# A ring of five weight units, stage boundaries that split units ahead of the norm, another opening, and an attention stage with its rotary key on GpSimd

## The reference, cut to what matters

```python
for i in range(DEPTH):
    f = swiglu(rmsnorm(h, ffn1_pre_g[i]), ffn1_w_in[i], ffn1_w_down[i])     # 1024 -> 2 x 2816 -> 1024
    h = h + 0.5 * rmsnorm(f, ffn1_post_g[i])
    hn = rmsnorm(h, mix_pre_g[i])
    if i % 2 == 0:   # gated MLP over chunks beside a state space scan, one output projection
        mixed = jnp.concatenate([ya, yb], axis=-1) @ hyb_w_out[j]
    else:            # latent attention: 16 heads, a rotary key shared by all of them
        mixed = mla_attention(hn, ..., cos, sin)
    h = h + rmsnorm(mixed, mix_post_g[i])
    f = swiglu(rmsnorm(h, ffn2_pre_g[i]), ffn2_w_in[i], ffn2_w_down[i])
    h = h + 0.5 * rmsnorm(f, ffn2_post_g[i])
    gate = jax.nn.sigmoid(rmsnorm(h, ple_pre_g[i]) @ ple_w_gate[i])
    h = h + rmsnorm(gate * (p[i] @ ple_w_proj[i]), ple_post_g[i])
```

## Time and profile before

| | |
|---|---|
| three runs | 1171.07, 1170.84, 1170.70 us (median 1170.84) |
| the profiled execution | 1170.79 us, span 1169.0 |
| granted clock of TensorE, mean over the span | 0.995 of full speed |
| TensorE busy | 1123.9 us, 5780 matmuls |
| VectorE, ScalarE, GpSimd busy | 819.4, 566.4, 114.3 us |
| read from HBM | 204.29 MB, 176 GB/s |

### The profile page before, as it was taken

The page is one execution under the profiler, slowest core; times in us unless marked ns, Lnnn a source line. Parts: engine busy times, 40 slices in busy tenths (PEclk is TensorE's granted clock), DMA queues, the critical chain, the costliest instruction groups (busy, mean ns, idle before and its releaser), DMA issues.

```text
span 1169.0 us, 15408 instructions
## 1 busy us (share of the span) xinstructions
PE 1123.9 (96%) x5780; PEld 945.5 (81%) x5780; DVE 819.4 (70%) x1027; ACT 566.4 (48%) x671; POOL 114.3 (10%) x139
## 2 busy tenths in 40 slices
PE   7999999999899999999998999999989999999997
PEld 4888887788787788888777888887878878888875
DVE  5767777677786677677765777768865576776775
ACT  5444445567433644444555444445554554444453
POOL 4000000201600300000123000003100030000012
PEclk9999999999999999999999999999999999999999
DMA  7654554744342564645455655553622356555441
GB/s 269 239 216 173 186 183 146 283 163 158 112 163 108 186 219 180 213 172 190 154 195 197 216 176 183 184 212 108 216 108 73 109 188 216 178 182 205 166 169 54
DMA packets 30546, 206.05 MB, mean 176 GB/s; under 512 B 3504, under 2 KB 3536, under 8 KB 7072
## 3 DMA queue, kind: packets, MB, share of 16 engines
q1 hardware_dynamic: 27216, 194.00, 46.3%
q0 software_dynamic: 3280, 11.35, 3.0%
HBM read 204.29 MB, written 1.05 MB: 176 GB/s over the span
## 4 chain that ended last, share of the span: by engine, by line
PE 83%; DVE 9%; POOL 2%; ACT 2%; issue 1%; DMA 1%; DVEq 0%; POOLq 0%; ACTq 0%
PE PS L505 23%; PE PS L202 15%; PE PS L203 14%; PE PS L204 14%; PE PS L508 12%; DVE WL L178 4%; DVE hn L341 1%; DVE h L317 1%; DVE X L381 1%; DMA QG<-pre_g 1%; PE PS L354 1%; PE PS L1606 1%; PE PS L1607 1%; ACT junk L271 1%; ACT WH L172 0%
## 5 line engine op out<-in xcount | busy, mean ns | idle before, releaser
L178 DVE TENSOR_TENSOR WL<-raw,WH 128x2048 fp32r<-128x2048 f32 x182 | 418.1, 2299 | 147.2 <-ACT WH L172 147.1
L172 ACT ACTIVATE WH<-raw 128x2048 fp32r<-128x2048 f32 x183 | 349.0, 1908 | 133.5 <-PE PS L204 127.6
L505 PE MATMUL PS<-X,WH 128*128 128x512 f32 x1152 | 288.4, 392 | 0.0
L505 PEld LDWEIGHTS PS<-X,WH 128*128 128x128 f32 x1152 | 209.1, 189 | 39.0 <-DVE actb L619 0.2
L508 PEld LDWEIGHTS PS<-X,WL 128*128 128x128 f32 x1152 | 157.2, 190 | 11.2
L508 PE MATMUL PS<-X,WL 128*128 128x256 f32 x1152 | 160.6, 282 | 0.0
L202 PE MATMUL PS<-WH,X 128*128 128x512 f32 (+1 forms) x352 | 140.6, 400 | 9.1 <-DVE X L381 6.6
L204 PE MATMUL PS<-WL,X 128*128 128x512 f32 (+1 forms) x352 | 137.2, 390 | 0.0
L203 PE MATMUL PS<-WH,X 128*128 128x512 f32 (+1 forms) x352 | 137.1, 389 | 0.0
L202 PE MATMUL PS<-WH,BH 128*128 128x512 f32 x288 | 113.4, 394 | 0.0
L203 PE MATMUL PS<-WH,BL 128*128 128x512 f32 x288 | 112.5, 391 | 0.0
(11 more groups left out here) (265 smaller groups left out, 1365.8 us busy)
## 6 DMA issues: line engine op xcount, KB each, us to landing
raw<-stream SPq DMA_DIRECT2D x183, 1024.0 KB, 4.8
QG<-pre_g POOLq DMA_DIRECT2D x8, 512.0 KB, 8.0
PG<-post_g POOLq DMA_DIRECT2D x8, 512.0 KB, 6.8
h<-x SPq DMA_DIRECT2D x2, 512.0 KB, 7.6
out<-h SPq DMA_DIRECT2D x4, 256.0 KB, 2.0
wsT<-gm_w POOLq DMA_DIRECT2D x1, 512.0 KB, 10.5
gm_g<-gm_g POOLq DMA_DIRECT2D x1, 512.0 KB, 11.0
gm_b<-gm_b POOLq DMA_DIRECT2D x1, 512.0 KB, 13.9
```

Of the source, the lines that this page charges most:

```text
L172: act.activation(WH[:, n % RING, :], raw[:, n % RING, :], ACT.Copy).then_inc(sem("w_hi"), 1)
L178: dve.tensor_tensor(WL[:, n % RING, :], raw[:, n % RING, :], WH[:, n % RING, :], ALU.subtract).then_inc(sem("w_lo"), 1)
L505: pe.matmul(PS[:, bank, :], wh[:, kt, cols], X[:, kt, :, :].rearrange("p a n -> p (a n)"), start=kt == 0, stop=False)
```

## The change

It touches five things.

*The ring.* It has five slots in place of three, and `WL` is placed over the same bytes as `raw`, so the low part is written over the raw data. A load waits until unit n-5 has been used (`w_used`); ACT's split waits for the load alone. The loops of the feed-forward stages are written out; splits come one or two units earlier.

*Boundaries.* On DVE one split goes ahead of `behind` and one between x's low part and the second `behind`; on ACT one more unit is split ahead of x's high part. The sum of the squares' halves (`post_mean`) moves from GpSimd to DVE. After a ple stage the gains no longer wait for the squares. `lagged` takes a lead of 2: second tokens stand two units behind, and their transposes at the third unit (in hybrid by `first_gemms`, the first two projections in one such order). The transposes of the next stage's first tokens come in two halves between the last products. In a ple stage a gate block stands between the two projections; ACT splits up to first+6 before it loads the sigmoid's table, up from first+4.

*The opening.* x is transposed as it is, and the gains are applied by ACT as a scale (`qg_cols`, one column for each 128 of width) when it makes the high part; units 0 and 1 are loaded and split by halves. ACT's first table load stands behind the wait for the transposes and for `qg_cols` in the new order; before it stood ahead of every wait. The idle products start on a `zeros` tile of their own wait, 7 and 8 in place of 16 and 4.

*Attention.* The rotary key is copied by ACT (`krs`) and rotated for both token blocks at once on GpSimd; its transposes come as a piece of their own behind the queries. The half split on GpSimd is gone. The order of pieces is queries, then keys; K2 stands behind the first scores, K3, R1, Q2, Q3 in the first two steps of the head loop. `out_unit(5, 1)` and `out_unit(6, 0)` move to the last steps.

```diff
-RING = 3
+RING = 5
...
+        WL = place("WL", [P, RING, UNIT], f32r, offset=base)
         WH = place("WH", [P, RING, UNIT], f32r)
-        WL = place("WL", [P, RING, UNIT], f32r)
...
-        def load_unit(sp, n, k=None, step=0):
+        def load_unit(sp, n):
             if n >= RING:
-                sp.wait_ge(sem("w_hi"), unit_at(n - RING + 1, k, step))
-                sp.wait_ge(sem("w_lo"), unit_at(n - RING + 1, k, step))
...
-            sp.dma_start(raw[:, n % RING, :], src).then_inc(sem(f"raw{n % RING}"), 16)
...
+                sp.wait_ge(sem("w_used"), n - RING + 1)
+            sp.dma_start(raw[:, n % RING, :], a["stream"][n, :, :]).then_inc(sem(f"raw{n % RING}"), 16)
...
-            if n >= RING:
-                act.wait_ge(sem("w_used"), unit_at(n - RING + 1, k, step))
+            act.wait_ge(sem(f"raw{n % RING}"), 16 * (n // RING + (1 if n % RING > 1 else 0)))
             act.activation(WH[:, n % RING, :], raw[:, n % RING, :], ACT.Copy).then_inc(sem("w_hi"), 1)
...
+        def lagged(units, lead=1):
...
+            order = []
+            for j in range(len(units) + lead):
+                if j < len(units):
+                    order.append((units[j], 0))
+                if j >= lead:
+                    order.append((units[j - lead], 1))
...
+            if stages[s][0] != "ple":
+                dve.wait_ge(sem("post_sq"), 4 * s + 2 * t + b + 1)
...
+        def post_mean(dve, s, t):
+            dve.wait_ge(sem("post_sq"), 4 * s + 2 * t + 2)
+            if stages[s][0] == "ffn":
+                dve.wait_ge(sem("pre_rs"), 2 * s + t + 1)
+            dve.tensor_scalar(col(s, t, POST_RS), col(s, t, POST_SQ), col(s, t, POST_SQ + 1),
+                              col(s, t, POST_EPS) if stages[s][0] == "ffn" else EPS, ALU.add, ALU.add)\
+               .then_inc(sem("post_ms"), 1)
...
+        def first_x_high(act, t, a_):
+            if (t, a_) == (0, 0):
+                act.wait_ge(sem("qg_cols"), 16)
+            act.wait_ge(sem("x_tr"), 2 * t + a_ + 1)
+            for q in range(4):
+                kt = 4 * a_ + q
+                ins = act.activation(XH[:, kt, tok(t)], PS[:, x_bank(0, t, a_), q * P:(q + 1) * P], ACT.Copy,
+                                     scale=qg_cols[:, kt:kt + 1])
+            ins.then_inc(sem("x_hi"), 1)
...
+            split_to(m + 2)
             x_high(act, s, 0)
-            split_to(m + 1)
-            if s:
-                post_square(act, s - 1, 1)
+            post_square(act, s - 1, 1)
             pre_square(act, s, 0)
-            split_to(m + 3 if stages[s][0] == "ple" else m + 2)
+            split_to(m + 3)
...
+        def opening_act(act, done):
+            act.wait_ge(sem("consts"), 1)
+            first_x_high(act, 0, 0)
+            first_part_hi(act, 0, 0)
+            first_x_high(act, 0, 1)
+            first_part_hi(act, 0, 1)
+            pre_square(act, 0, 0)
+            first_part_hi(act, 1, 0)
+            first_x_high(act, 1, 0)
...
+            load_table(act, ACT.Silu)
...
+            split_to(m + 1)
             behind(dve, s - 1, 0)
...
-            split_to(m)
             x_low(dve, s, 0)
-            split_to(m + 1)
+            if stages[s][0] != "mla":
+                split_to(m + 2)
             behind(dve, s - 1, 1)
             x_low(dve, s, 1)
             if stages[s][0] != "mla":
-                split_to(m + 2)
+                split_to(m + 3)
...
+            order = lagged(range(4), 2) if s else [(j, t) for j in range(4) for t in range(2)]
...
+                    if s and (j, t) == (2, 0) and q % 2 == 0:
+                        transpose_x(pe, s, 1, (q // 2,))
...
+            def projected(t, middle=None):
...
-                wide(pe, u, t, 4 + 2 * t, p_hi, p_lo, 0, True, True)
-            for j, t in [(0, 0), (0, 1), (1, 0), (2, 0), (3, 0), (1, 1), (2, 1), (3, 1)]:
+                wide(pe, u, t, 4 + 2 * t, p_hi, p_lo, 0, True, True, middle=middle)
+            def gate(j, t):
                 if j == 0:
                     x_there(pe, s, t, 1)
-                wide(pe, u + 1 + j, t, 2 * t, XH, XL, 2 * j, j == 0, j == 3, "ple_gate" if j == 3 else None,
-                     middle=(lambda: transpose_x(pe, s, 1)) if (j, t) == (0, 0) else None)
+                wide(pe, u + 1 + j, t, 2 * t, XH, XL, 2 * j, j == 0, j == 3, "ple_gate" if j == 3 else None)
+            pe.wait_ge(sem("p_lo"), i + 1)
+            projected(0)
+            gate(0, 0)
+            projected(1, lambda half: transpose_x(pe, s, 1, (half,)))
+            for t in range(2):
+                for j in range(1 - t, 4):
+                    gate(j, t)
...
-            split_to(first[s] + 4)
+            split_to(first[s] + 6)
             load_table(act, ACT.Sigmoid)
         def ple_dve(dve, s, done, split_to):
-            split_to(first[s] + 4)
+            split_to(first[s] + 5)
...
+        ROPE0, V00, V01, ROPE1, V10, V11, Q0, Q1, R0, K0, K1, K2, K3, Q2, R1, Q3 = range(16)
         PIECES = [(PA, "turn", None), (PB, "act", None), (PC, "act", None), (PD, "turn", 2), (PB, "act", None),
-                  (PC, "act", 3), (PA, "act", None), (PB, "dve", None), (PC, "act", None), (PD, "dve", 4),
-                  (PA, "act", None), (PB, "dve", 5), (PC, "act", None), (PD, "dve", None), (PA, "act", None),
-                  (PB, "dve", 6)]
+                  (PC, "act", 3), (PA, "act", None), (PB, "dve", 4), (PA, "act", None), (PC, "act", None),
+                  (PB, "dve", None), (PA, "act", None), (PB, "dve", 5), (PA, "act", None), (PB, "dve", None),
+                  (PB, "act", 6)]
...
+            wait_emptied(K0)
+            pe.wait_ge(sem("ml_krT"), 1)
             scores(0)
             scores(1)
-            turned(Q3, u + 6, 2, 4, 0)
-            wait_emptied(R1)
+            keys(2)
             for j in range(8):
                 if j == 1:
+                    wait_emptied(Q2)
+                if j == 2:
                     wait_emptied(Q3)
                 transpose_probabilities(2 * j)
                 if j < 7:
                     scores(2 * j + 2)
-                if j:
+                if j == 0:
+                    keys(3)
+                if j == 1:
+                    transpose_ropes(1)
+                if 0 < j < 7:
                     out_unit(j - 1, 0)
+                if j == 7:
+                    out_unit(5, 1)
                 transpose_probabilities(2 * j + 1)
                 if j < 7:
                     scores(2 * j + 3)
                 weighted_values(2 * j)
-                if j == 7:
...
-                if j > 1:
+                if j == 0:
+                    queries(2)
+                if j == 1:
+                    queries(3)
+                if 1 < j < 7:
                     out_unit(j - 2, 1)
...
+                weighted_values(2 * j + 1)
+            out_unit(6, 0)
...
             take(V11)
+            take(Q0)
+            split_to(u + 7)
+            rotary_key()
+            take(R0)
             take(K0)
-            split_to(u + 6)
-            take(K2)
-            split_to(u + 7)
-            take(Q0)
-            take(R0)
-            take(Q2)
             load_table(act, ACT.Exp)
...
+            split_to(u + 2)
+            latent_means(0)
             dve.wait_ge(sem("ml_cg"), 32)
             latents(0)
-            dve.wait_ge(sem("ml_half"), 1)
-            split_lo_half(dve, u + 2, 1).then_inc(sem("w_lo"), 1)
-            done[0] = u + 3
             latents_low(0)
             split_to(u + 3)
+            latent_means(1)
             latents(1)
-            split_to(u + 4)
             latents_low(1)
             turn(0)
+            split_to(u + 4)
             turn(1)
             split_to(u + 5)
+            take(Q1)
+            split_to(u + 6)
             take(K1)
-            take(K3)
-            split_to(u + 6)
-            take(Q1)
             split_to(u + 7)
-            take(R1)
+            dve.wait_ge(sem("ml_cm"), 1)
...
+                if j < 2:
+                    take((K3, R1)[j])
+                split_to(u + 7 + j)
...
+            pool.wait_ge(sem("ml_kr"), 2)
+            pool.wait_ge(sem("ml_cn"), 2)
+            x0, x1 = krs[:, :, 0:HALF], krs[:, :, HALF:ROPE]
+            pool.tensor_tensor(kw[:, 0, :, :], x0, cosT[:, :, :], ALU.mult)
+            pool.tensor_tensor(kw[:, 1, :, :], x1, sinT[:, :, :], ALU.mult)
+            pool.tensor_tensor(kw[:, 2, :, :], x1, cosT[:, :, :], ALU.mult)
+            link(pool, "pool_chain", pool.tensor_tensor(kw[:, 3, :, :], x0, sinT[:, :, :], ALU.mult))
+            for twice in range(2):
+                lo = 384 + ROPE * twice
+                pool.tensor_tensor(cn[:, :, lo:lo + HALF], kw[:, 0, :, :], kw[:, 1, :, :], ALU.subtract)
+                ins = pool.tensor_tensor(cn[:, :, lo + HALF:lo + ROPE], kw[:, 2, :, :], kw[:, 3, :, :], ALU.add)
+            ins.then_inc(sem("ml_krr"), 1)
...
+            sp.dma_start(qg_cols[:, :], a["pre_g0"]).then_inc(sem("qg_cols"), 16)
+            load_part(0, 0)
```

(7 more changed lines are left out.)

562 lines of the change are left out of this document (287 added, 275 removed).

## The result

| | before | after |
|---|---|---|
| median of four runs, us | 1170.95 (1170.70 to 1171.50) | 1160.32 (1156.69 to 1160.80) |
| profiled execution, span | 1170.79, 1169.0 | 1160.76, 1159.0 |
| granted clock, mean | 0.995 | 0.988 |

The ratio is 0.9902, with a 95% interval of 0.9881 to 0.9922: 10.6 us faster by the medians, 10.0 by the spans. The forecast was 1162.6. The mean clock is lower than before; the one run of 1156.69 had a clock of 0.994, the three around 1160.3 of 0.988.

A forecast was written before the change was run, and what follows sets the result against it. TensorE was busy 1123.9 of 1169.0 us, leaving some 45 us of waits to win. Terms 3.9 + 0.5 + 1.1 + 1.2 + 3.6 - 3.7 + 1.5 = 8.1 gave 1162.6 us, own range 1159 to 1166, whole range 1154.5 to 1167.5.

The forecast's parts named there:

- Opening: Kernel start: first product at 10.5 instead of 14.67, four blocks done at 23.7 instead of 27.6; gain 3.9 us.
- Ring and steady loops: Feed-forward loops: units land with 13 us to spare and the dropped loop registers cost no time; change 0.
- Feed-forward to embedding: Start of both embedding stages: a gate block in front removes the second projection's wait; gain 1.8 us, twice.
- Embedding to feed-forward: End of the embedding stage: ACT splits through first+6 before the sigmoid's table, so sigmoids start at its end; loss 3.7 us.
- The rival of 0.22: Embedding stage: ACT is not late, so the time is 6.9 us better, 1155.7; chance 0.22.
- The first failed term: the hybrid: Boundaries into and out of the hybrid stage: one split goes ahead of everything; gains of 0.5 and 1.1 us.
- The second: attention: Attention and the stage ahead of it: earlier rotary queries and filled waits gain 2.7 us, or 1.5 after the clock.
- The clock: Two new attention waits of 2.6 and 2.9 us: slow products behind them cost 0.6 each, 1.2 us in all.
- The rule against the change: Attention: GpSimd shares SBUF interfaces with VectorE, so eight rotary-key pieces on GpSimd contend with the first queries' rotation.
- the rival of a collision: Attention: eight GpSimd pieces stretch the first rotation by 3.4 us and the first queries wait, giving 1166; chance 0.08.

The follow-up runs named there:

- table_early: The changed kernel with one tiny activation of the copy's kind at the opening, so ACT's first table load falls into idle time: 1158.30 us.
- ring4: The changed kernel with four slots in the ring instead of five, nothing else: 1256.13 us, ratio 1.0726.
- gate_early: The changed kernel with one embedding-stage product block (unit first+1, tokens 128 to 255) moved earlier on TensorE: 1150.22 us.
- hyb_out: gate_early with the last low part of the hybrid stage's output operand ahead of the split of first+25 on DVE: 1152.51 us.
- mean_pool: gate_early with the mean of the squares' halves formed on GpSimd again instead of on DVE: 1148.45 us.
- latents_first: gate_early with attention's split of first+2 on DVE put behind the first latents instead of ahead of their means: 1149.88 us.
- means_first: gate_early with the two means of attention's first latents ahead of the split of first+2 on DVE: 1151.51 us.

## Why the prediction was right, and where it was not

By the table of stretches, with the prediction's terms put into them:

| stretch | predicted | measured |
|---|---|---|
| opening | +3.9 | +3.8 |
| over the hybrid (+0.5, +1.1) | +1.6 | -0.6 |
| over the embedding (+1.8, -3.7) | -1.9 | -1.0 |
| attention and its two boundaries (+1.5, +1.2) | +2.7 | +4.8 |
| behind the last feed-forward (+1.8), end | +1.8 | +3.1 |
| sum | +8.1 | +10.0 |

The stretch over the embedding splits once more: up to that stage's end E the change gains 2.7 (1.8 forecast), from E on it loses 3.7, as forecast. That the sum came within 2 us is in part luck: the hybrid stage was 2.2 too high, attention 2.1 too low and the ways into the two embedding stages 0.9 and 1.3 too low. TensorE's rows behind E, which is 603.5 in the changed kernel, first tokens and second:

```profile
609.46 1.12 PE L367 MATMUL PS<-ident,hn 128*128 128x128 f32 x4 [5.79 <-DVE hn L351]
...
612.08 0.77 PE L189 MATMUL PS<-WH,X 128*128 128x512 f32 x1
```

```profile
620.33 0.63 PE L367 MATMUL PS<-ident,hn 128*128 128x128 f32 x4 [0.35 <-DVE hn L351]
```

- **Opening.** The chain is right, and table_early shows the table load's part of it. The 3.9 is not what its terms give: from 5.7 the load, the copies and the splits add up to 10.1, not 10.5, and 10.5 + 10.9 + 0.9 + 0.4 + 1.5 is 24.2, not 23.7, so 3.4. Measured are 10.48 for the first product, 0.5 and 0.7 for the two waits (the second was put at 1.5), and 24.0 for the end of the fourth block. That the slips bring the term to within 0.1 of the 3.8 measured is luck.
- **Ring and steady loops, 0.** Right. The blocks take 149.3 us as before. ring4 shows what the fifth slot is for, which the prediction did not price: without it the same order of splits costs 96 us.
- **Feed-forward to embedding, +1.8 twice.** Right in kind, small in size: the waits of 0.3, 0.3, 1.6 and 0.3 of each are gone but for 0.2, where 0.5 was to come in.
- **Embedding to feed-forward, -3.7.** The step held in each link: ACT idle for the load of first+6, the sigmoids at the stage's end (forecast at E, found at E+0.3), the first product at E+8.6 (forecast E+8.0), the second tokens at E+16.8 (forecast E+16.7), shown from two sides. The rival of 0.22, that ACT is not late, is out; its price of 6.9 for the absence of this loss was right too (6.6 in gate_early).
- **The first failed term: the hybrid.** It was given two boundaries (+1.6) and nothing inside. Inside, the third split ahead of CL cost 1.2 (hyb_out), and two waits for WL of 0.6 in all are new; what causes those was not tested. At the boundaries TensorE's waits fell from 1.2 to 1.1 and from 1.8 to 1.5, 0.5 in place of 1.6, because the mean on DVE holds the second tokens' hn: with it back on GpSimd (mean_pool) the three waits for hn, 2.4 in all, are gone. The prediction had this cost at 0.5 for the first tokens and 0.7 for the second.
- **The second: attention, under-sized.** The 2.7 is not what the terms beside it give: 2.1 - 2.2 + 1.8 + 1.7 + 1.2 is 4.6. The boundary from feed-forward to attention was left out of the sum too; there the waits for hn and X fell from 1.9 to 0.7. TensorE waits at the latents for 1.9 and 0.9 in two pieces, where I had 2.6, and for pr 2.0, where I had 2.9. The clock fell behind the first in this execution and cost some 3.1 (0.51 for 6.4 us) where I took 0.6, and not at all behind the second. In gate_early, with no half clock there, the two stretches are 319.3 us against 327.0 before, so at full clock this part gains 7.7: the half clock hid how far the term was too small.
- **The clock.** The 1.2 was a sum over two waits, right for neither. The rows here, 0.52 behind 5.8 us of idle time and 0.51 behind 1.9 and 0.6, agree with what the Trainium skill says of an array that is throttled unless activity releases it ("TensorE: Matmul & The Clock Gate", What's actually happening). But the reading that every such wait is followed by slow products is not borne out: at the latents gate_early's wait of 2.0 and latents_first's of 1.5 are followed by none, and in the hybrid stage mean_pool's wait of 3.5 is not either. A mean price per wait is the best that I can put in a sum.
- **The rule against the change.** The eight pieces on GpSimd took 0.32 or 0.33 each, as at the forecast's lower rows, and hurt nothing: they ran from 819.80 to 822.2, and the rotation on DVE began at 824.64.

```profile
819.80 0.32 POOL L2004 TENSOR_TENSOR kw<-krs,cosT 128x64 f32<-128x64 f32 x1 [0.93 <-DVE cn L1898]
```

So the rival of a collision did not come true here, for want of overlap. The sharing itself is real, and it goes both ways. In the earlier trace rows GpSimd's half split started first, and DVE's piece ended with it (815.81 and 815.77). In means_first and mean_pool DVE's split started first, and GpSimd was held (2.67 for 0.70, 1.90 for 0.38). In each of the three the one that started later waited.

## What to carry to other kernels

A split or a load is free only while the engine that makes it has nothing wanted behind it: with in-order engines, ask of every prefetch that is moved forward which use frees its slot, and whether that use comes before the work queued behind it. A product block moved on TensorE, with nothing changed on ACT, was worth 6.6 us. Price a stall by what is late next: half clock ahead of a wait that another engine ends cost 0.5 of the 3.3 us that were expected from it, and half clock behind a wait in the hybrid stage cost about 1.6. When medians jump with the clock, read an edit from its own stretch of the trace, and say that this is one execution. Two errors that cancel make a sum look better than its terms: compare term by term.

## What the runs showed of the hardware

- GpSimd was held while VectorE ran a tensor_tensor of two SBUF inputs (128x2048, 2.28 us) that had started 0.2 and 0.6 us before: a power of 128x2 took 2.67 instead of 0.70, a sum of 128x1 took 1.90 instead of 0.38, and with the split moved away the power took 0.70 again. The other way round, a VectorE piece of two SBUF inputs (128x32) that started 1.3 us into GpSimd's half split took 1.14 and ended with it; one with a single SBUF input, the other from PSUM, took 0.18 beside the same half split.
- The granted clock after like waits differs from one profiled execution to another: after 1.9 and 0.6 us of waiting at the latents it was 0.51 for 6.4 us in the changed kernel and 1.00 in gate_early, whose waits there are 2.0 and 0.6. With 36 or 30 small transposes in the idle stretch it was 1.00 in both places that were tried, in one profile of the first and two of the second; in the second (3.5 us, hybrid stage) it was also 1.00 in one of twelve profiles without them.
- ACT's first table load (1.28 us) stood behind the waits of the first activation where that has three of them (constants, `qg_cols`, transposes: 5.60 in the changed kernel), and ahead of the wait where it has one (0.80 before, 0.79 in table_early, whose small activation itself ran at 2.46).
